# Sums of squares of queries and keys: from one-column products per chunk to rows of sums for all heads

## The reference

```
q = (rms_norm(c_q, g_qa) @ w_qb).reshape(B, S, MLA_HEADS, QK_HEAD)
kv = (rms_norm(c_kv, g_kva) @ w_kvb).reshape(B, S, MLA_HEADS, QK_NOPE + V_HEAD)
k = jnp.concatenate([k_nope, jnp.broadcast_to(k_r[:, :, None, :], ...)], axis=-1)
q = rms_norm(q, g_qn)      # x * rsqrt(mean(x * x over 192) + 1e-6) * g
k = rms_norm(k, g_kn)
```

## Time and profile before

| | |
|---|---|
| median of 3 runs | 1635.32 us (1631.61 to 1635.99) |
| the profiled execution, its own time | 1637.03 us |
| its span (first to last instruction) | 1635.7 us |
| mean granted TensorE clock | 0.994 of full |
| TensorE busy | 1610.8 us (98%) |
| the stage of the change | about 74 to 112 us |

### The profile page before, as it was taken

The page is one execution under the profiler, slowest core; times in us unless marked ns, Lnnn a source line. Parts: engine busy times, 40 slices in busy tenths (PEclk is TensorE's granted clock), DMA queues, the critical chain, the costliest instruction groups (busy, mean ns, idle before and its releaser), DMA issues.

```text
span 1635.7 us, 17948 instructions
## 1 busy us (share of the span) xinstructions
PE 1610.8 (98%) x7508; PEld 1318.6 (81%) x7508; DVE 885.4 (54%) x1178; ACT 650.7 (40%) x783; POOL 11.7 (1%) x25
## 2 busy tenths in 40 slices
PE   7999999999999999999999999999998999999998
PEld 6787777888888888888798888888886888888887
DVE  5646656774444441257655644354444787766313
ACT  4536657543232221155443433223334453444212
POOL 1000000000000000000000000000000000000000
PEclk9989999999999999999999999999998999999999
DMA  5311110213333323323221133222323232232232
GB/s 166 97 52 58 46 52 27 71 59 116 103 103 103 96 86 103 103 97 103 89 99 52 56 105 103 82 89 88 103 77 103 78 104 82 99 103 92 101 103 78
DMA packets 117216, 144.25 MB, mean 88 GB/s; under 512 B 6017, under 2 KB 103648, under 8 KB 117136
## 3 DMA queue, kind: packets, MB, share of 16 engines
q1 hardware_dynamic: 115712, 139.88, 26.1%
q0 software_dynamic: 1232, 3.16, 0.6%
q10 hardware_dynamic: 192, 0.07, 0.0%
HBM read 140.99 MB, written 2.10 MB: 87 GB/s over the span
## 4 chain that ended last, share of the span: by engine, by line
PE 95%; ACT 2%; DVE 2%; DMA 1%; issue 0%; SPq 0%; POOL 0%; DVEq 0%; ACTq 0%
PE bank L380 28%; PE bank L382 28%; PE bank L381 28%; PE bank L913 1%; PE bank L676 1%; PE bank L694 1%; PE bank L675 1%; PE bank L739 1%; PE bank L896 1%; PE bank L615 1%; PE bank L441 1%; ACT slab_hi L1873 1%; PE bank L734 1%; DMA slab_raw<-in_w_in 0%; PE bank L685 0%
## 5 line engine op out<-in xcount | busy, mean ns | idle before, releaser
L380 PE MATMUL bank<-h_hi,slab_hi 128*128 128x512 f32 x1192 | 473.9, 398 | 5.2 <-DVE h_lo L1072 3.1
L1067 DVE TENSOR_TENSOR slab_lo<-slab_raw,slab_hi 128x2048 fp32r<-128x2048 f32 x130 | 296.1, 2278 | 334.3 <-ACT slab_hi L1873 333.7
L382 PE MATMUL bank<-h_hi,slab_lo 128*128 128x512 f32 x1192 | 466.1, 391 | 0.0
L381 PE MATMUL bank<-h_lo,slab_hi 128*128 128x512 f32 x1192 | 465.8, 391 | 0.0
L1873 ACT ACTIVATE slab_hi<-slab_raw 128x2048 fp32r<-128x2048 f32 x130 | 246.5, 1897 | 175.1 <-DMA slab_raw<-in_w_down 142.6
L380 PEld LDWEIGHTS bank<-h_hi,slab_hi 128*128 128x128 f32 x1192 | 224.8, 189 | 58.4 <-issue 10.3
L381 PEld LDWEIGHTS bank<-h_lo,slab_hi 128*128 128x128 f32 x1192 | 225.0, 189 | 47.9 <-issue 2.2
L382 PEld LDWEIGHTS bank<-h_hi,slab_lo 128*128 128x128 f32 x1192 | 224.8, 189 | 47.5
L1109 DVE TENSOR_TENSOR tmp<-bank,x_rstd_rows 128x512 f32<-128x512 f32 x98 | 66.6, 687 | 95.7 <-PE bank L382 95.6
L380 PE MATMUL bank<-slab_hi,h_hi 128*128 128x256 f32 (+1 forms) x224 | 74.8, 334 | 0.0
L382 PE MATMUL bank<-slab_hi,h_lo 128*128 128x256 f32 (+1 forms) x224 | 73.6, 328 | 0.0
(11 more groups left out here) (417 smaller groups left out, 2142.7 us busy)
## 6 DMA issues: line engine op xcount, KB each, us to landing
slab_raw<-in_w_in SPq DMA_DIRECT2D x40, 1024.0 KB, 5.0
slab_raw<-in_w_up SPq DMA_DIRECT2D x33, 1024.0 KB, 5.0
slab_raw<-in_w_down SPq DMA_DIRECT2D x22, 1024.0 KB, 4.9
slab_raw<-in_w_gate SPq DMA_DIRECT2D x11, 1024.0 KB, 5.2
slab_raw<-in_w_o SPq DMA_DIRECT2D x4, 1024.0 KB, 4.9
slab_raw<-in_w_ple_gate SPq DMA_DIRECT2D x4, 1024.0 KB, 5.0
slab_raw<-in_w_ret_o SPq DMA_DIRECT2D x4, 1024.0 KB, 4.9
slab_raw<-in_w_sgu_o SPq DMA_DIRECT2D x4, 1024.0 KB, 4.9
```

The costliest lines, as they stand in the source:

```text
L380: T.matmul(ps, a_hi, b_hi, start=start, stop=False, skip_group_check=skip)
L381: T.matmul(ps, a_hi, b_lo, start=False, stop=False, skip_group_check=skip)
L382: return T.matmul(ps, a_lo, b_hi, start=False, stop=stop, skip_group_check=skip)
L1067: V.tensor_tensor(w_lo[j][:, 0:n], raw[j][:, 0:n], w_hi[j][:, 0:n].bitcast(F32), ALU.subtract).then_inc(slab_lo, 1)
```

## The change

The sums are turned round: the squares become the moving operand (512 tokens), and a selector with 8 columns the stationary one. Column r of the selector holds ones (or a half of ones), the others zeros, so that each product adds the sums of one tile to row r of an 8 x 512 tile in bank 7; the rows are q0 to q3 and k0 to k3. Since these products use the shorter float, the squares are split: ScalarE writes the high part of the squares (`sq_hi`), VectorE the rest (`sq_lo`), and TensorE takes two products for each group. ScalarE copies the 8 rows to SBUF, four transposes on TensorE turn them to 32 columns (`qk_cols`), and the root reads these.

```
     small = np.concatenate([ident, ones, cols], 1)      # cols grows from 16 to 47 columns
...
+    select = sb("row_selectors", [P, NCOL - 8], F32R)
+    head_row_of = [select[:, 7 - r:15 - r] for r in range(2 * HEADS)]
+    pair_rows_of, key_rows = [select[:, 22 - 2 * r:30 - 2 * r] for r in range(2)], select[:, 31:39]
...
-        jobs = [(HEADS * TT, lower_halves)] + [(hd, ones[:, 0:1]) for hd in range(HEADS)]
-        jobs += [(0, halves), (2, halves)] + [(HEADS * TT + hd, ones[:, 0:1]) for hd in range(HEADS)]
+        jobs = [key_rows] + head_row_of[0:HEADS] + pair_rows_of + head_row_of[HEADS:]
         def sum_squares(n):
-            at, which = jobs[n]
-            T.wait_ge(qk_squared, n + 1)
-            for t in range(TT):
-                c = at + HEADS * t
-                ins = T.matmul(sums[:, c:c + which.shape[1]], tmp[n % 4][:, chunk[t]], which, start=n == 0 and t == 0,
-                               stop=n >= 5, skip_group_check=True)
+            T.wait_ge(qk_sq_lo, n + 1)
+            T.matmul(sums[0:2 * HEADS, :], jobs[n], sq_hi[n % 3], start=n == 0, stop=False, skip_group_check=True)
+            ins = T.matmul(sums[0:2 * HEADS, :], jobs[n], sq_lo[n % 3], start=False, stop=n == 10, skip_group_check=True)
             passed(("qk_sum", n), ins)
...
         for t in range(TT):                                # the value tiles, TensorE
...
+            if t == 2:
+                T.wait_ge(tile["qk_sums"].free, tile["qk_sums"].value)
+                ps = take("qk_cols", 7)
+                for j in range(TT):
+                    ins = T.transpose(ps[:, 8 * j:8 * j + 8], tmp[5][0:2 * HEADS, chunk[j]], ident[0:2 * HEADS, 0:2 * HEADS])
+                whole("qk_cols", ins)
...
+        def squares_lo(n):                                 # VectorE
+            V.wait_ge(qk_sq_hi, n + 1)
+            V.tensor_tensor(sq_lo[n % 3], tmp[n % 2], sq_hi[n % 3].bitcast(F32), ALU.subtract).then_inc(qk_sq_lo, 1)
...
+        squares_lo(0)
         rotated(0, kr_raw[:, 0, :])
         split(6)
         for t in range(6):
             copied(("q", t), q_nope[:, t, :] if t < HEADS else q_rope[:, t - HEADS, :])
+            if t:
+                squares_lo(t)
+        squares_lo(6)
...
         split(7)
         for t in range(HEADS):
             copied(("k", t), k_nope[:, t, :])
-        t = tile["qk_sums"]
+            if t:
+                squares_lo(6 + t)
+        squares_lo(10)
+        t = tile["qk_cols"]
         V.wait_ge(t.free, t.value)
...
         def squares(n, src):                               # ScalarE
-            if n >= 4:
-                A.wait_ge(psum_ready, mark["qk_sum", n - 4])
-            A.activation(tmp[n % 4], src, ACT.Square).then_inc(qk_squared, 1)
+            if n >= 2:
+                A.wait_ge(qk_sq_lo, n - 1)
+            A.activation(tmp[n % 2], src, ACT.Square).then_inc(qk_squared, 1)
+            if n >= 3:
+                A.wait_ge(psum_ready, mark["qk_sum", n - 3])
+            if n == 2:
+                A.wait_ge(rope_out, 1)
+            A.wait_ge(qk_squared, n + 1)
+            A.activation(sq_hi[n % 3], tmp[n % 2], ACT.Copy).then_inc(qk_sq_hi, 1)
+        A.activation(select[:, :], ccol[:, 8:NCOL], ACT.Copy).then_inc(selected, 1)
...
-        root("qk_sums", rcol[:, :], tile["qk_sums"].ps[:, 0:32], QK)
-        for t in range(TT):
-            copied(("v_mla", t), v_mla[:, t, :])
+        A.activation(tmp[5][0:2 * HEADS, :], t.ps[0:2 * HEADS, :], ACT.Copy).then_inc(t.free, 1)
+        copied(("v_mla", 0), v_mla[:, 0, :])
+        copied(("v_mla", 1), v_mla[:, 1, :])
+        root("qk_cols", rcol[:, :].rearrange("p (s t h) -> p s t h", s=2, t=TT),
+             tile["qk_cols"].ps[:, 0:32].rearrange("p (t s h) -> p s t h", s=2, t=TT), QK)
+        copied(("v_mla", 2), v_mla[:, 2, :])
+        copied(("v_mla", 3), v_mla[:, 3, :])
```

More of the change, by code:

```diff
@@ L31 @@
 F2T = 2 * F1 // P
+NCOL = 47
 ROWS = {}
@@ L51, in const_tables @@
     inv = (10000.0 ** (-np.arange(0, ROPE, 2) / ROPE))
-    cols = np.zeros((P, 16))
+    cols = np.zeros((P, NCOL))
     cols[:, 0] = EPS
@@ L60, in const_tables @@
     cols[:, 7] = i
-    cols[:, 8] = i < 64
-    cols[:, 9] = i >= 64
-    cols[:, 12:16] = (i < 64)[:, None]
+    cols[:, 8 + 7] = 1.0
+    cols[:, 23 + 7] = i < 64
+    cols[:, 23 + 8] = i >= 64
+    cols[:, 39 + 4:39 + 8] = (i < 64)[:, None]
     small = np.concatenate([ident, ones, cols], 1)
@@ L153, in program @@
     tmp_end = top[0]
-    cs = sb("const_small_sb", [P, 2 * P + 16])
+    cs = sb("const_small_sb", [P, 2 * P + NCOL])
     dcol = sb("decay_cols", [P, 8 * 10])
@@ L157, in program @@
     eps_col, halfpi_col, freq_col, sign_col = (ccol[:, k:k + 1] for k in range(4))
-    halves, lower_halves = ccol[:, 8:10], ccol[:, 12:16]
+    select = sb("row_selectors", [P, NCOL - 8], F32R)
+    head_row_of = [select[:, 7 - r:15 - r] for r in range(2 * HEADS)]
+    pair_rows_of, key_rows = [select[:, 22 - 2 * r:30 - 2 * r] for r in range(2)], select[:, 31:39]
     arena = (top[0] + BLK - 1) // BLK * BLK
@@ L183, in program @@
     x_diag = slot("x_diagonals", 17, 1, shape=[P, TT, P])
+    sq_hi, sq_lo = ([sb(f"sq_{n}{j}", [P, S], F32R, at=tmp_end - (8 - j - odd) * BLK)[:, :] for j in (2, 6, 4)]
+                    for odd, n in enumerate(("hi", "lo")))
     x_sq = sb("x_squares", [P, TT, D], at=tmp_end - 8 * BLK)
@@ L262, in program @@
     rope_in, rope_out = sem("rope_in"), sem("rope_out")
+    selected, qk_sq_hi, qk_sq_lo = sem("selectors"), sem("qk_squares_hi"), sem("qk_squares_lo")
     qk_squared, qk_rstd, head_diag, head_done = sem("qk_squared"), sem("qk_rstd"), sem("head_diag"), sem("head_scaled")
@@ L597, in tensor_program @@
         T.wait_ge(masks_landed, 16)
+        T.wait_ge(selected, 1)
         sums = take("qk_sums", 7)
@@ L1981, in scalar_program @@
             squares(7 + t, k_nope[:, t, :])
-        root("qk_sums", rcol[:, :], tile["qk_sums"].ps[:, 0:32], QK)
-        for t in range(TT):
-            copied(("v_mla", t), v_mla[:, t, :])
+        t = tile["qk_sums"]
+        A.wait_ge(psum_ready, t.done)
+        A.activation(tmp[5][0:2 * HEADS, :], t.ps[0:2 * HEADS, :], ACT.Copy).then_inc(t.free, 1)
[5 more added lines that the diff above has]
+        copied(("v_mla", 3), v_mla[:, 3, :])
         split(8)
```

## The result

| | before | after |
|---|---|---|
| median of 20 runs each | 1634.03 us (1631.45 to 1638.60) | 1636.79 us (1635.07 to 1639.58) |
| ratio after to before, 95% interval | | 1.0015 (1.0008 to 1.0022) |
| the profiled execution, time and span | 1637.03, 1635.7 us | 1636.61, 1635.3 us |
| start of the rotary key's product, start of head_row(0) | 73.75, 109.89 | 73.55, 110.06 |
| the stage between them | 36.14 us | 36.51 us |

The changed kernel is 0.15% slower, 2.5 us (1.3 to 3.6), while TensorE is busy 7.5 us less.

The account below looks back on a forecast made before the run. TensorE, busy 98% of the span, was taken as the bound. Savings of 9.6 us less 7.3 of waits put head_row(0) at 107.7; 3.2 of half clock made 110.9, +1.0 on the median: 1636.3 us, range 1631.8 to 1640.0.

Parts of the forecast that it names:

- The three waits: TensorE's new waits ahead of q0's group, k0's group and head_row(0): 7.3 us in all (2.4 + 3.6 + 1.3).
- TensorE's account: Thin groups removed, 22 products at 0.23 us and transposes of 0.44 added: TensorE gains 6.5 us, 9.6 at full clock.
- First wait: Ahead of the second group (q0's squares): the gap grows from 0.92 to 3.3 us, the group starting at 82.5.
- Second wait: Ahead of k0's group of sums: a new gap of 3.6 us, the group starting at K + 8.7.
- Third wait: Ahead of head_row(0): copies, table load, root, reciprocal and diagonal make TensorE wait 1.3 us.
- The clock: After each of two gaps over 3 us, half clock costs 0 to 2.3 us, taken as 1.6: 3.2 together.
- The base: Difference of +1.0 us, reckoned against the profiled execution of 1637.03 us, put on the kernel before's median of 1635.32.
- K: Start of k0 on TensorE, from which the times around k0's squares are counted; forecast at 88.5 at full clock.
- the full clock: Rival: the clock stays at full through the stage, -2.2 us, 1633.1 us; chance 0.19.
- The long half clock: Rival: half clock lasts as long as before after each gap, 5.1 us per gap, +8.0, 1643.3 us; chance 0.11.
- The wait-free account: Rival: the other engines keep ahead of TensorE and no waits come, 1625 to 1629 us; chance 0.06.

Follow-up runs that it names:

- e5: The changed kernel with slab 6's high and low parts alone moved, right behind slab 5's; 1633.08 us.
- e6: The changed kernel with slab 7's high and low parts alone moved behind the squares; 1633.16 us.
- e7: The changed kernel with the root's table load alone moved ahead of the wait for the sums; 1635.68 us.
- e2: The changed kernel with 12 unread products ahead of the second group of sums and 15 ahead of k0's, filling the gaps; 1633.36 us.
- e10: The kernel before, unchanged, in three more profiled executions; 1630.52, 1634.88 and 1636.78 us.
- e9: The changed kernel with both slabs and the table load moved, plus the rotary key's last two operations and the gains moved on VectorE; 1626.44 us.
- e4: The changed kernel with the high part of the squares only, without the rest and 11 of the 22 products; 1629.57 us.
- e8: The kernel before with 4 unread products of 512 columns ahead of the second group of sums, filling its gap; 1631.12 us.

## Why the prediction was right

The time: +1.0 was forecast on 1635.32, and 1636.79 measured, against 1634.03 for the kernel before over 20 runs; the result lies in the range, and on the side that was forecast. The three waits, who ends them and the two low stretches came as forecast. That the sum of 1636.3 came within 0.5 us is partly luck: the base was 1.3 us above the median of 20 runs, and the difference was 1.5 us too small by the ratio.

- *TensorE's account.* A group at 0.23 us per product with 8 stationary columns: 0.23 and 0.24 measured. Transposes 0.44: 0.34 measured (107.00 to 107.34), with about 0.2 more on the products beside them. Right.
- *First wait.* 3.3 forecast, 2.97 measured; start 82.5 forecast, 82.00 measured. Part of the difference is that the stage began 0.2 earlier. The rest is a misreading of the row at 77.14 of the kernel before: there VectorE could have gone on near 76.94 (0.61 us behind the row at 76.33), and slab_lo waited for ScalarE's slab_hi, which ended at 77.11 (row below). So the subtraction added 0.08 us ahead of slab_lo (77.02 less 73.55, against 77.14 less 73.75) and not 0.36. Moving slab 6 leaves 0.61 us of this wait (e5). ScalarE in the kernel before:

```profile
75.21 1.90 ACT L1873 ACTIVATE slab_hi<-slab_raw 128x2048 fp32r<-128x2048 f32 x1
```

- *Second wait.* K + 8.7 forecast; k0 started at 89.29 and its group at 98.01, K + 8.72, and slab_lo and the copies stand where the sum had them (K + 3.66, K + 5.87). Right, and moving slab 7 leaves 0.84 us (e6).
- *Third wait.* 1.3 forecast, 1.22 measured, and it is the table load (e7). By the 1.38 us of drain that the Trainium skill counts (ScalarE: Activation LUTs, "What ACT_TABLE_LOAD costs") the root would have come at 109.97, an estimate; it came at 108.61, 0.02 after the load, and the load itself started 0.01 after the copy ahead of it. The measurement decides: no drain is seen here.
- *The clock.* Two low stretches at 1.6 us each were forecast, 1.4 and 1.7 measured, and e2 gives 2.8 us back by filling the gaps. Right in size, but the way to 1.6 was in part luck. Its ground was one gap elsewhere in the program, with 4.6 us of dense work at half clock behind it, and 1.6 was a choice between 0 and 2.3 with the reason that a part of the stretch may pass in the gap. Measured, a stretch was 3.4 us long in all, with 0.6 us of the first and nothing of the second in the gap, and e7 shows that after 2.80 us the clock can stay up.
- *The base.* This is the term that was mis-sized. The sum was made against an execution of the kernel before in which the clock's low stretch was at its longest (36.14 us of stage), and the difference was then put on the median. e10 shows stages of 31.50 and 34.72 too; the mean of the four is 34.66, 1.9 us below the changed kernel's one stage of 36.51. The new kernel seems to pay more regularly: over the kernels that keep one or both of its long gaps (after, e5, e6, e7) the clock fell at five of six, and its 20 runs lie in 4.5 us, those of the old one in 7.2. So the difference is +2.5 and not +1.0; with one trace of the changed kernel, how the last 0.6 us divides isn't shown. The prediction named the weakness itself, in its range (the median may sit on either side of a low stretch).

Of the rivals, the full clock's stage (-2.2) is what e2 made (-2.5). The long half clock didn't come: the longest low stretch of the stage with the wide products is 3.4 us. The wait-free account is what e9 comes near to: 26.99 us, where 25.7 (0.90 for the swap, 14 tiles at 1.38, 22 products at 0.23, 0.44) would be without any wait.

## What to carry to other kernels

Saving time on the bounding engine by giving its neighbours a longer chain pays only as far as the neighbours' queues are free at that moment: look for the long operations that stand ahead of the chain (here a 2.2 us slab part, twice, and a table load), and move them when they aren't needed yet. The moves alone were worth 4 to 5 us to the old kernel and 8 to 9 to the new one; the change without them was a loss. Where a short gap decides whether the clock falls, one profile of the kernel before is a sample of several cases, so take the base from the times and not from the one trace.

## What the runs showed of the hardware

- The granted clock fell after a gap of 0.92 us between thin products in three of four executions of the kernel before, once for about 7 us and twice for about 10. Between products of 512 columns it stayed at full after gaps of 1.61 and 2.02 us (e4). It fell at 2.81 us (after) and 2.80 (e6) and didn't at 2.80 in another trace (e7), and it fell at 3.46 us in all three traces (after, e5, e7).
- Products whose result nobody reads, put into a gap, made a program faster by 3.4 us (e2) and by 2.3 us (e8).
- Low stretches differ in length from place to place: 3.4 us each in this stage of the changed kernel, but 10.2 us around the gap of 3.14 us near 1260 us, there in all 14 traces of before, after and the experiments.
- A stationary operand of 8 columns loads in 0.09 us where 128 columns take 0.19, but a product of 512 moving columns with it costs the same 0.23 us. The rows (shortest, median and longest in ns) are of before and of after:

```profile
L615 PEld LDWEIGHTS bank<-const_small_sb,tmp x88: 186/192/333, 77.2 to 106.9; 128*128 128x128 f32 x88
L621 PEld LDWEIGHTS bank<-sq_hi,row_selectors x11: 85/88/131, 77.0 to 104.9; 128*8 128x8 f32 x11
```
